# Moving the last adaLN pass of a hybrid decoder step from the key scores to S5, in half panels

## The chip, the core and the metric

One NeuronCore of a Trainium2 chip runs the whole program; the other cores are idle. The metric is device microseconds of one execution, the median of the runs. The engines are TensorE (PE, with its weight loads as PEld), VectorE (DVE), ScalarE (ACT), GpSimd (POOL) and SyncE (SP). The last two issue most of the DMAs here, POOL on queue q0 and SP on queue q1; both are worked off by the same 16 DMA engines. Everything is float32. A float32 matmul shows as two MATMUL instructions in the trace, so 8 matmuls are "x16".

## The reference

A two-layer decoder step is computed for one prompt of 256 tokens and eight samples of one token each, with width 1024 and shared weights. Layer 0 is attention (MoBA with 8 heads, and NSA with compressed, selected and window branches), layer 1 is an S5 state-space layer with a GLU. Each is followed by a squared-ReLU MLP. Each of these four sub-layers has its own conditioning:

```python
def adaln(c, w, b):
    m = (jax.nn.silu(c) @ w + b)[:, None, :]
    return jnp.split(m, 3, axis=-1)          # shift, scale, gate
def modulate(x, g, shift, scale):
    return rms_norm(x, g) * (1 + scale) + shift
def mlp_sublayer(x, c, g, ada_w, ada_b, w1, w2):
    shift, scale, gate = adaln(c, ada_w, ada_b)
    h = modulate(x, g, shift, scale)
    return x + gate * (jnp.square(jax.nn.relu(h @ w1)) @ w2)
```

Here `c` has 9 rows (prompt and samples), and each `w` is 1024 x 3072, 12 MB. Four such passes are computed, numbered 0 (attention), 1 (MLP of layer 0), 2 (S5) and 3 (MLP of layer 1). The result of pass 3 is needed only by the last MLP: by its norm, its gates and nothing earlier.

## The kernel before

The program is one straight list of instructions for each engine, ordered by hand; semaphores with counted values (class `Signals`) tie the lists together. The stages that matter here, in order, with their time in the profile:

- **MoBA values** (280 to 372 us). SP loads 64 units of 256 KB (128 rows of one cache page) into 8 slots `kv`. TensorE's `moba_pv(r)` uses 8 units a round. Behind rounds 0 to 2 stands the conditioning pass 2 (`ada(2, ...)`), between rounds 3 to 7 stand pair steps of the prompt's attention (`pair_scores`, `pair_rest`).
- **Key scores** (375 to 441 us). 24 units: 16 of selected keys (SP loads units 0, 1, 4, 5 of each 8, POOL gathers 2, 3, 6, 7), then 8 of window keys (SP, in runs of 512 bytes). For each unit n TensorE transposes (`turn_keys`), ACT evacuates, TensorE scores (`score_keys`). `beside_keys(n)` puts other work between the units.
- **Pair steps of NSA** (453 to 515 us) with values by SP, then the **output projection** (two panels, `w_out`), norm 1, and **MLP 0** (557 to 803 us).
- **S5** (803 to 877 us): norm 2 (DVE multiplies, ACT adds the shift), copies of `hT` into `U[half]`, `states_in(half)` on TensorE, then a DVE chain (`turn_in`, `states`), with `y_of(k)` on TensorE for the outputs of each half.
- **GLU** (878 to 937 us), norm 3, **MLP 1** and the output.

A conditioning pass loads six panels of 1024 x 512 (2 MB) into the ring of 4 slots, multiplies each (8 matmuls with `cT` as weights in four column groups, 32 rows each), ACT copies the row out (`ada_evac`), and 16 small matmuls turn it back into columns (`turn_back`). DVE's `mods_evac` adds the bias and gain.

Pass 3 stands in the key scores: its panels have ring numbers 28 to 33, its matmuls follow units 9, 11, 13, 15, 18 and 21 (`ADA3_AT`). POOL's queue issues in this order: pass 2's six panels, pass 3's panels 0 to 3, the gathered key units, pass 3's panels 4 and 5, the two panels of `w_out` (numbers 34 and 35), the first four MLP panels. A load waits until its slot is used: `mm_done` grows by 4 for each ring panel, and the first MLP panels wait for `4 * SEQ["w_out"]`.

In S5 the ring is cut anew: its lower half holds 4 MLP-sized panels of 1 MB (`panels`), and `PANEL` numbers them in order, w1 and w2 of layer 0, the GLU's 8, then layer 1. Panel n is loaded when panel n - 4 is used. Ahead of `states_in(0)` TensorE waits for the whole norm:

```python
normed(2)
pe.wait_ge(N.out_free, 16)
pe.wait_ge(N.s5_b_ev, 4 * LAG)
pe.wait_ge(N.s5_c_ev, LAG)
...
pe.wait_ge(N.u_dve, 1)
states_in(0)
pe.wait_ge(N.s5_b_ev, 4 * LAG + 1)
states_in(1)
```

## Time and profile before

| | |
|---|---|
| median of 3 runs | 1185.12 us (1183.18 to 1186.55) |
| the profiled execution | 1189.66 us, span 1187.9 us |
| mean granted TensorE clock | 0.908 of full speed |
| busy in the span | PE 1026.6 us (86%), DVE 421.4 (35%), ACT 252.4 (21%), POOL 121.5 (10%) |
| chain that ended last | PE 69%, DMA 11%, DVE 11%, ACT 4% |
| DMA | 215.10 MB, mean 181 GB/s |

The span runs from the first to the last instruction, and the execution's own time has some 1.8 us around it. A timeline row gives the start, the time it covers, the engine, the program line (L), the operation with its operands, the count of merged instructions, and in brackets how long the engine stood idle before it and what ended that. The chain follows the last instruction back through what released it, so it shows which of several waits counted. In a window row PEclk is the share of full clock that TensorE was granted, 1.00 for 2.4 GHz and 0.50 for 1.2 GHz. The mean DMA rate hides stages: at some the DMA engines are full, at others nearly idle.

### The profile page before, as it was taken

The page shows a single profiled execution, that of the slowest core. Times are in us where ns is not written, and L with a number is a line of the kernel's source. Part 1 is how long each engine was busy: PE and PEld are TensorE (multiplying, and loading weights), DVE is VectorE, ACT ScalarE, POOL GpSimd, SP SyncE. Part 2 cuts the span into 40 slices and gives each one's busy share as a digit, 9 for nine tenths or more (in the row PEclk, how much of TensorE's full clock was granted, in tenths as well). Part 3 has the DMA queues.
Part 4 walks back from the last instruction along what each step waited for, and adds up shares of the span by engine and source line. Part 5 has one row for each costly group of instructions (what it writes and reads, how often), then busy time and mean ns, then how long its engine had stood idle before and what let it go on. Part 6 is the DMA issues. An engine that isn't in the chain of part 4 may idle for free.

```text
span 1187.9 us, 20856 instructions
## 1 busy us (share of the span) xinstructions
PE 1026.6 (86%) x8308; PEld 748.3 (63%) x8308; DVE 421.4 (35%) x893; ACT 252.4 (21%) x546; POOL 121.5 (10%) x154
## 2 busy tenths in 40 slices
PE   4868999945878878997999999994679799999998
PEld 2556433422323545676888888884568588878886
DVE  0434049878042344533797310006931300000000
ACT  3234121102033432422213322005021211100000
POOL 2000000101103310000111111020002011111110
PEclk9779989977898875898999999997689899999999
DMA  9984549989997794303744434441014334543440
GB/s 326 340 280 130 179 156 346 354 301 376 404 341 235 251 307 140 89 19 60 259 147 136 143 135 142 142 140 39 4 47 141 108 106 144 154 159 120 162 144 36
DMA packets 106762, 215.10 MB, mean 181 GB/s; under 512 B 20464, under 2 KB 53040, under 8 KB 106585
## 3 DMA queue, kind: packets, MB, share of 16 engines
q0 software_dynamic: 38464, 147.96, 36.9%
q1 hardware_dynamic: 66314, 63.05, 16.6%
q10 hardware_dynamic: 1904, 2.94, 0.7%
q8 instruction: 60, 0.98, 0.3%
q14 instruction: 20, 0.16, 0.0%
HBM read 210.63 MB, written 7.48 MB: 184 GB/s over the span
## 4 chain that ended last, share of the span: by engine, by line
PE 69%; DMA 11%; DVE 11%; ACT 4%; SPq 2%; issue 2%; DVEq 0%; ACTq 0%; POOL 0%; POOLq 0%
PE psum L1194 20%; PE psum L1203 19%; DMA sb_arena<-in_cache_moba_kv 7%; PE psum L1386 5%; PE psum L624 4%; PE psum L772 2%; PE psum L1178 2%; PE psum L808 2%; DVE sb_sq L1932 2%; PE psum L683 2%; DVE sb_sq L1936 2%; DMA sb_arena<-in_state_nsa_win 2%; DMA sb_ring<-in_attn_ada_w 1%; PE psum L696 1%; DMA sb_arena<-in_cache_nsa_kv 1%
## 5 line engine op out<-in xcount | busy, mean ns | idle before, releaser
L1194 PE MATMUL psum<-sb_hT,sb_ring 128*128 128x264 f32 x1024 | 234.3, 392 | 13.3 <-ACT sb_hT L1433 6.8
L1203 PE MATMUL psum<-sb_arena,sb_ring 128*128 128x264 f32 x1024 | 229.1, 386 | 2.6 <-DVE sb_arena L2180 2.4
L1194 PEld LDWEIGHTS psum<-sb_hT,sb_ring 128*128 128x128 f32 x1024 | 197.7, 194 | 48.0 <-issue 6.8
L1203 PEld LDWEIGHTS psum<-sb_arena,sb_ring 128*128 128x128 f32 x1024 | 194.2, 190 | 36.3 <-issue 3.2
L624 PE MATMUL psum<-sb_cst,sb_arena 128*128 128x128 f32 (+4 forms) x457 | 77.4, 307 | 34.1 <-DMA sb_arena<-in_cache_nsa_kv 8.0
L624 PEld LDWEIGHTS psum<-sb_cst,sb_arena 128*128 128x128 f32 (+4 forms) x457 | 55.1, 154 | 54.0 <-issue 24.4
L2187 DVE SCALAR_TENSOR_TENSOR sb_xT<-psum,sb_mods,sb_xT 128x256 f32<-128x256 f32 (+1 forms) x16 | 7.7, 483 | 223.2 <-PE psum L1203 223.2
L808 PE MATMUL psum<-sb_ring,sb_hT 128*128 128x512 f32 (+1 forms) x192 | 79.4, 566 | 0.0
L683 PE MATMUL psum<-sb_ring,sb_cT 128*32 128x512 f32 x384 | 57.4, 708 | 11.3 <-DMA sb_ring<-in_attn_ada_w 10.1
L2180 DVE TENSOR_TENSOR sb_arena<-sb_arena x16 | 19.7, 1256 | 127.4 <-ACT sb_arena L1671 108.5
L808 PEld LDWEIGHTS psum<-sb_ring,sb_hT 128*128 128x128 f32 x192 | 35.5, 190 | 44.2 <-issue 39.8
L1386 PE MATMUL psum<-sb_sq,sb_ring 128*128 128x264 f32 x256 | 58.2, 386 | 1.1 <-ACT sb_sq L1712 1.1
L567 POOL DMA_DIRECT2D sb_ring<-in_mlp_w x28 | 24.8, 884 | 317.8 <-PE psum L1194 146.7
L1386 PEld LDWEIGHTS psum<-sb_sq,sb_ring 128*128 128x128 f32 x256 | 48.6, 190 | 9.5 <-ACT sb_sq L1712 1.3
L902 PE MATMUL psum<-sb_arena 128*32 128x512 f32 x128 | 43.7, 733 | 10.4 <-DMA sb_arena<-in_cache_moba_kv 10.2
L574 POOL DMA_DIRECT2D sb_ring<-in_mlp_w x32 | 28.3, 884 | 210.5 <-PE psum L1203 146.0
L1932 DVE TENSOR_TENSOR sb_sq<-sb_arena 128x512 f32<-128x512 f32 x64 | 42.0, 689 | 11.8 <-DMA sb_arena<-in_cache_moba_kv 5.6
L1936 DVE TENSOR_REDUCE sb_sq<-sb_sq 128x1024 f32 x32 | 39.0, 1220 | 4.8 <-DVE sb_sq L1932 1.3
L1848 DVE COPY sb_arena<-psum 64x256 f32<-64x256 f32 x64 | 27.3, 427 | 33.8 <-PE psum L624 32.5
L683 PEld LDWEIGHTS psum<-sb_ring,sb_cT 128*32 128x32 f32 x384 | 12.9, 124 | 37.4 <-issue 35.1
L1655 ACT COPY sb_arena<-psum 32x2048 f32<-32x2048 f32 x16 | 29.7, 1857 | 27.5 <-PE psum L624 27.2
L1671 ACT ACTIVATE sb_arena<-psum 128x264 f32 x32 | 12.5, 391 | 104.0 <-PE psum L1194 104.0
(414 smaller groups left out, 1098.6 us busy)
## 6 DMA issues: line engine op xcount, KB each, us to landing
sb_ring<-in_mlp_w POOLq DMA_DIRECT2D x64, 1024.0 KB, 6.1
sb_arena<-in_cache_moba_kv SPq DMA_DIRECT2D x128, 256.0 KB, 7.4
sb_ring<-in_mlp_ada_w POOLq DMA_DIRECT2D x12, 2048.0 KB, 13.3
sb_ring<-in_attn_ada_w POOLq DMA_DIRECT2D x6, 2048.0 KB, 22.5
sb_ring<-in_ssm_ada_w POOLq DMA_DIRECT2D x6, 2048.0 KB, 16.9
sb_ring<-in_attn_w_in POOLq DMA_DIRECT2D x5, 2048.0 KB, 11.5
sb_arena<-in_cache_nsa_kv SPq DMA_DIRECT2D x64, 128.0 KB, 2.6
sb_ring<-in_s_w_glu POOLq DMA_DIRECT2D x16, 512.0 KB, 5.3
```

The lines of the kernel that those rows point to most:

```text
L574: pool.dma_start(panels[:, j, :].rearrange("p (f c) -> p f c", f=8), w2[:, 8 * j:8 * j + 8, DS(it * 256, 256)]).then_inc(mlp_full_at[j], 16)
L624: return nc.tensor.transpose(out, in_, ident[0:rows, 0:rows])
L683: last = mm(mm_banks[i % len(mm_banks)][group(k), 0:512], cT[:, k, :], ring[:, seq % SLOTS, 512 * k:512 * k + 512], start=(k < 4), stop=(k ...
L808: last = mm(bank[3 * (p % 2) + t][:, 0:w], hT[:, k, P * t:P * t + P], ring[:, seq % SLOTS, w * k:w * k + w], start=(k == 0), stop=(k == KC ...
L902: mm(bank[5][rows, 0:512], p_of(half, r // 2, pg), kv[:, seq % KVS, :], start=(r == 0 and pg < 2), stop=(r == 7 and pg == 7)).then_inc(kv_ ...
L1194: last = mm(bank[m % 4][:, 0:T], panels[:, j, 256 * k + P * ch:256 * k + P * ch + P], hT[:, k, :], start=(k == 0), stop=(k == KC - 1))
L1203: last = mm(bank[2 * pair + c][:, 0:T], panels[:, j, 256 * f + P * c:256 * f + P * c + P], actT[:, 8 * j + f, :], start=(j == 0 and f == 0 ...
L1386: last = mm(bank[b][:, 0:T], panels[:, seq % SLOTS, 256 * k + P * zi:256 * k + P * zi + P], yT[:, k, :], start=(k == 0), stop=(k == KC - 1))
L1655: nc.scalar.copy(BT[32 * i:32 * i + 32, e].rearrange("p r k n -> p (r k n)"), psum[32 * e:32 * e + 32, 4:8, :].rearrange("p a c -> p (a c) ...
L1848: last = cp(pairs_of(n, e, 1), turned_of(n, e, 1))
L1932: tt(prod[:, 512 * (pg % 2):512 * (pg % 2) + 512], kv[:, pg, :], qb[:, DS(b, 1), :].rearrange("p b c -> p (b c)"), ALU.mult).then_inc(kv_f ...
L1936: last = red(sraw_b[:, DS(b, 1), 8 * (pg - 1):8 * (pg + 1)].rearrange("p b c -> p (b c)"), prod.rearrange("p (h d) -> p h d", d=64), AX, A ...
```

## The change

Pass 3 leaves the ring, POOL's early queue and `beside_keys`. It becomes 12 half panels of 1024 x 256 (1 MB), numbered 32 to 43 in `PANEL`, between MLP 0 and the GLU, whose numbers move up by 12. `w_out` takes ring numbers 30 and 31; the first MLP panels wait only for the end of pass 2.

TensorE's list in S5: halves 0 to 5 stand ahead of `states_in(0)`, which no longer waits for the whole norm; three turns and halves 6 to 9 stand between the samples' matmuls and `y_of(4)`; halves 10 and 11 behind `y_of(7)`; the last three turns in the GLU after its second panel. Two halves share a PSUM bank, and ACT evacuates them in pairs (`late_evac`) into rows of `work` (`late_rows`). ACT no longer makes the copies of lags 0 and 1 for the second half of `U`; DVE makes them, as it did for the first half. `mods_evac(3)` moves from the key scores' end to the GLU's end. `tmp8x` and `ss8` move within `cT`, whose columns 0 to 8 the pass still needs.

```diff
 SLOTS = 4
-SEQ = dict(ada0=0, cmp=6, cmp_p=20, ada2=22, ada3=28, w_out=34)
+SEQ = dict(ada0=0, cmp=6, cmp_p=20, ada2=22, w_out=30)
 W_IN_SEQ, ADA1_SEQ = (8, 9, 11, 13, 15, 17), (10, 12, 14, 16, 18, 19)
 W_ORDER = (0, 4, 1, 5, 2, 6, 3, 7)
-ADA3_AT = (9, 11, 13, 15, 18, 21)
-MLP_START = 36
-PANEL = dict(w1_0=0, w2_0=16, glu=32, w1_1=40, w2_1=56)
+W_OUT_START = 28
+MLP_START = 30
+PANEL = dict(w1_0=0, w2_0=16, ada3=32, glu=44, w1_1=52, w2_1=68)
...
         K3 = work[:, 0:768].rearrange("p (k d c) -> p k d c", k=8, d=LAG - 1)
+        late_rows = [work[:, 768 + 512 * (j % 4):1280 + 512 * (j % 4)] for j in range(6)]
         us = work[:, 3072:3328].rearrange("p (k e b) -> p k e b", k=8, e=4)
...
         xlast = work[:, 3968:4032]
-        ss8 = cT[:, 0, 8:16]
+        ss8 = cT[:, 0, 24:32]
         U = [sqf[:, c:c + 1024].rearrange("p (k e t) -> p k e t", k=4, e=4) for c in (1024, 0)]
...
             load_ada(SEQ["ada2"], I["ssm_ada_w"][0])
-            load_ada(SEQ["ada3"], I["mlp_ada_w"][1], 0, 4)
             selected = I["cache_nsa_kv"][0].rearrange("n p a h d -> n p (a h d)")
...
                                        ).then_inc(selected_full[u % KVS], 16)
-            load_ada(SEQ["ada3"], I["mlp_ada_w"][1], 4, 6)
             for i in range(2):
...
                 if layer == 0:
-                    pool.wait_ge(N.mm_done, 4 * SEQ["w_out"])
+                    pool.wait_ge(N.mm_done, 4 * W_OUT_START)
                     for j in range(SLOTS):
...
             load_mlp(0)
+            for i in range(12):
+                n = PANEL["ada3"] + i
+                pool.wait_ge(N.mm_done, mlp_done(n - SLOTS + 1))
+                pool.dma_start(panels[:, n % SLOTS, :].rearrange("p (k c) -> p k c", k=KC),
+                               by_rows(I["mlp_ada_w"][1])[:, :, 256 * i:256 * i + 256]).then_inc(mlp_full_at[n % SLOTS], 16)
             for i in range(8):
...
         GAINS = ((MQ, 8, 0), (MK, 8, 1), (NQ, 8, 2), (KSEL, 2, 4), (KWIN, 2, 5))
-        ADA_SEQ = tuple(tuple(SEQ[name] + i for i in range(6)) if name in SEQ else ADA1_SEQ for name in ("ada0", "ada1", "ada2", "ada3"))
+        ADA_SEQ = tuple(tuple(SEQ[name] + i for i in range(6)) if name in SEQ else ADA1_SEQ for name in ("ada0", "ada1", "ada2"))
         GAIN_AT = (96, 120, 104, 128)
...
                     last.then_inc(N.pv_done, 1)
-                if n in ADA3_AT:
-                    i = ADA3_AT.index(n)
-                    ada(3, bank[0:1], bank[7], first=i, end=i + 1)
                 if n == 19:
...
             pe.wait_ge(N.win_log, 1)
-            pe.wait_ge(N.ada_row, 6 * 4)
             for h in range(NSA_H):
...
             pe.wait_ge(N.cp_ready, 1)
-            pe.wait_ge(N.mods_ready, 4)
             pe.wait_ge(N.bias_nsa, 16)
...
-            normed(2)
+            LATE_BANK = (4, 5, 7, 0, 6, 4)
+
+            def late_half(i):
+                seq = PANEL["ada3"] + i
+                pe.wait_ge(mlp_full_at[seq % SLOTS], mlp_full(seq))
+                c = TP * (i % 2)
+                for k in range(KC):
+                    last = mm(bank[LATE_BANK[i // 2]][group(k), c:c + TP], cT[:, k, :], panels[:, seq % SLOTS, TP * k:TP * k + TP],
+                              start=(k < 4), stop=(k >= 4))
+                last.then_inc(N.mm_done, 2)
+
+            def late_turn(j):
+                pe.wait_ge(N.ada_row, 18 + j + 1)
+                for ch in range(4):
+                    for g in range(4):
+                        c = 256 + (4 * j + ch) * 9
+                        last = mm(bank[7][32 * g:32 * g + 32, c:c + 9], late_rows[j][:, P * ch + 32 * g:P * ch + 32 * g + 32],
+                                  cst[:, C_SL:C_SL + 9], start=True, stop=True)
+                last.then_inc(N.ada_tr, 1)
+
             pe.wait_ge(N.out_free, 16)
...
             pe.wait_ge(N.s5_c_ev, LAG)
+            pe.wait_ge(N.s5_b_ev, 4 * LAG + 1)
+            for i in range(6):
+                late_half(i)
...
             states_in(0)
-            pe.wait_ge(N.s5_b_ev, 4 * LAG + 1)
+            normed(2)
+            pe.wait_ge(N.u_dve, 2)
+            pe.wait_ge(N.ada_row, 18 + 3)
             states_in(1)
...
             last.then_inc(N.us_mm, 1)
+            pe.wait_ge(N.u_free, 8)
+            for j in range(3):
+                late_turn(j)
+            for i in range(6, 10):
+                late_half(i)
             pe.wait_ge(N.x_done, 8)
...
                 y_of(k)
+            pe.wait_ge(N.y_ev, 7)
+            for i in range(10, 12):
+                late_half(i)
+            pe.wait_ge(N.ada_row, 18 + 5)
             for a in range(4):
...
                     pe.wait_ge(N.fin_ev, 2)
+                    for j in range(3, 6):
+                        late_turn(j)
                 if n:
...
                     nc.scalar.copy(keysT[:, n % 2, :], bank[2 + n % 2][:, 0:512]).then_inc(N.keys_ev, 1)
-                    if n + 1 in ADA3_AT:
-                        i = ADA3_AT.index(n + 1)
-                        ada_evac(3, bank[0:1], first=i, end=i + 1)
...
             last.then_inc(N.u_ready, 1)
-            u_half(1, range(LAG))
+            def late_evac(j):
+                act.wait_ge(N.mm_done, mlp_done(PANEL["ada3"] + 2 * j + 2))
+                if j >= 4:
+                    act.wait_ge(N.ada_tr, 18 + j - 3)
+                nc.scalar.copy(late_rows[j], bank[(4, 5, 7, 0, 6, 4)[j]][:, 0:512]).then_inc(N.ada_row, 1)
+
+            for j in range(3):
+                late_evac(j)
+            u_half(1, (2, 3))
+            late_evac(3)
+            late_evac(4)
             act.wait_ge(N.y_ev, 1)
...
                 f(yT[:, k, 0:TP], yT[:, k, 0:TP], ACT.Gelu_apprx_tanh).then_inc(N.gelu_ready, 1)
+            late_evac(5)
             act.wait_ge(N.fin_tr, 1)
...
                 dve.wait_ge(N.ada_tr, 6 * (n + 1))
-                src = bank[6 if n == 2 else 7]
+                src = bank[7][:, 256:] if n == 3 else bank[6 if n == 2 else 7]
                 then(tt(mods[:, n].rearrange("p c j -> p (c j)").rearrange("p (c j) -> p c j", j=9),
...
                     then(tt(tmp8x, xs, xs, ALU.mult))
-                    red(ss8, at(cT[:, 0, 0:], (1, 8), (32, 8)), AX, ALU.add).then_inc(N.x_ready, 1)
+                    red(ss8, at(cT[:, 0, 16:], (1, 8), (32, 8)), AX, ALU.add).then_inc(N.x_ready, 1)
                     scale_samples(n + 1)
...
-            tmp8x = cT[:, :, 0:8]
+            tmp8x = cT[:, :, 16:24]
...
-            mods_evac(3)
             dve.wait_ge(N.win_log, 1)
...
             for k in range(KC):
-                static_out(0, k, 4 * SEQ["w_out"] + k + 1, bank[k % 4])
+                static_out(0, k, 4 * W_OUT_START + k + 1, bank[k % 4])
             add_samples(0, 8)
...
             nc.vector.memset(X[:, :, :, 0:1], 0.0).then_inc(N.padded_ready, 1)
+            dve.wait_ge(N.h_ready, 24)
+            for i in range(2):
+                for e in range(4):
+                    last = cp(U[1][32 * i:32 * i + 32, :, e, :], hT[32 * e:32 * e + 32, 4:8, STEPS * i:STEPS * i + STEPS])
+            last.then_inc(N.u_dve, 1)
...
                 add_out(2, glu[:, n % 2, :], n, mods[:, 2, 16 + n], tmp8x[:, n, :])
+            mods_evac(3)
             add_samples(2, 24)
```

## Rows read from the trace of the kernel before

**Rows 1.** The page, part 3: DMA queue, kind: packets, MB, share of 16 engines.
```profile
q0 software_dynamic: 38464, 147.96, 36.9%
q1 hardware_dynamic: 66314, 63.05, 16.6%
```

**Rows 2.** Windows in the MoBA values: busy us by engine, PEclk, DMA share, GB/s.
```profile
314.00:320.00 6.00, 4.84 (x51) 1.73 (x51) 0.00 (x0) 0.00 (x0) 0.00 (x0) 1.00 1.03 404
...
350.00:356.00 6.00, 4.61 (x38) 2.21 (x38) 3.72 (x9) 3.42 (x11) 0.00 (x0) 1.00 0.64 198
```

**Rows 3.** Timeline of POOL's queue (start us, us, operation), 265 to 600 us.
```profile
309.71 0.88 POOL L510 DMA_DIRECT2D sb_ring<-in_mlp_ada_w  x1 [19.86 <-PE psum L683]
...
400.16 0.90 POOL L510 DMA_DIRECT2D sb_ring<-in_mlp_ada_w  x1
...
432.99 3.52 POOL L562 DMA_DIRECT2D sb_ring<-in_mlp_w  x4 [19.53 <-PE psum L683]
```

**Rows 4.** Chain of waits, 195 to 420 us: start us, us, what.
```profile
307.87 9.37 DMA sb_arena<-in_cache_moba_kv
...
364.03 6.44 DMA sb_arena<-in_cache_moba_kv
...
407.17 20.34 DMA sb_arena<-in_state_nsa_win
```

**Rows 5.** Timeline of TensorE in the MoBA values (L902 is their matmul).
```profile
329.59 2.20 PE L902 MATMUL psum<-sb_arena 128*32 128x512 f32 x12
...
334.99 1.05 PE L902 MATMUL psum<-sb_arena 128*32 128x512 f32 x2 [1.07 <-DMA sb_arena<-in_cache_moba_kv]
...
351.65 2.13 PE L902 MATMUL psum<-sb_arena 128*32 128x512 f32 x16
```

**Rows 6.** Timeline of SP's queue in the same stretch.
```profile
340.63 23.73 SPq L412 DMA_DIRECT2D sb_arena<-in_cache_moba_kv  x24
```

**Rows 7.** Timeline of TensorE in the key scores, 383 to 441 us.
```profile
400.78 1.92 PE L683 MATMUL psum<-sb_ring,sb_cT 128*32 128x512 f32 x16
402.50 0.46 PE L673 MATMUL psum<-sb_cst,sb_hT 128*32 128x9 f32 x32
...
427.55 1.12 PE L624 MATMUL psum<-sb_cst,sb_arena 128*128 128x128 f32 x4 [2.81 <-DMA sb_arena<-in_state_nsa_win]
...
429.05 3.62 PE L683 MATMUL psum<-sb_ring,sb_cT 128*32 128x512 f32 x16
...
440.51 2.13 PE L1108 MATMUL psum<-sb_arena 64*128 64x8 f32 x32 [0.67 <-ACT sb_arena L1536]
```

**Rows 8.** Windows and timeline of TensorE in the pair steps.
```profile
470.00:480.00 10.00, 10.00 (x44) 6.27 (x44) 3.41 (x8) 3.19 (x11) 0.00 (x0) 0.50 0.29 81
...
471.99 1.97 PE L624 MATMUL psum<-sb_cst,sb_arena 128*128 128x128 f32 x8
...
481.55 1.97 PE L624 MATMUL psum<-sb_cst,sb_arena 128*128 128x128 f32 x8
...
493.46 1.09 PE L624 MATMUL psum<-sb_cst,sb_arena 128*128 128x128 f32 x8
```

**Rows 9.** Timeline of all engines in S5, 799 to 895 us.
```profile
803.62 1.75 POOL L583 DMA_DIRECT2D sb_ring<-in_s_w_glu  x2 [5.36 <-PE psum L1203]
...
814.84 0.11 DVE L2337 MEMSET sb_arena<- 128x64 f32 x1
...
816.25 6.53 PE L1318 MATMUL psum<-sb_sq,sb_arena 128*32 128x64 f32 x256 [10.95 <-ACT sb_hT L1433]
...
866.52 1.50 PE L1330 MATMUL psum<-sb_hT,sb_arena 32*32 32x192 f32 x24 [7.74 <-DVE sb_arena L2408]
...
877.55 14.51 PE L1386 MATMUL psum<-sb_sq,sb_ring 128*128 128x264 f32 x64 [1.08 <-ACT sb_sq L1712]
```

**Rows 10.** The page, part 6 (KB each, us to landing); chain at 445 us.
```profile
sb_ring<-in_mlp_w POOLq DMA_DIRECT2D x64, 1024.0 KB, 6.1
...
445.61 0.30 DVE sb_mods L1755
```

## The prediction

> **What bounds the kernel now.** I read the page first, then the chain of waits in order of time, then the timelines of TensorE, of POOL and of SP in the two stretches that the change touches, and last the granted clock by stretch. TensorE carries most of the chain, but not in the first stretch. There the values of MoBA stream in by SP while POOL's queue carries weights. The page tells how the two queues differ: POOL's q0 moved 147.96 MB in 38464 packets (3.85 KB each), SP's q1 63.05 MB in 66314 (0.95 KB each) [rows 1]. From 314 to 320 us the 16 DMA engines are full (share 1.03, 404 GB/s), while at 350 to 356 they are not (0.64) [rows 2]. What fills them is the pass that leaves: POOL issues the first ada3 panel at 309.71 and three more soon after, 2 MB each [rows 3]. The chain then runs through DMA waits for kv units: one issued at 307.87 takes 9.37 us to land, one issued at 364.03, with no weights beside it, 6.44 us [rows 4]. In the key scores it is the same: ada3's last two panels are issued from 400.16 on [rows 3], the output projection's two behind them, and the fifth window unit, issued at 407.17, lands 20.34 us later [rows 4], when TensorE has waited for it until 427.55 [rows 7]. In S5 the bound is other: TensorE stands still for 10.95 us ahead of the first states matmul, waiting for ACT, and 7.74 us ahead of the second half's outputs, waiting for DVE [rows 9]. These are the gaps that the panels go into.
>
> **Part 1, the MoBA values.** 8 MB of ada3 leave the stretch from 310 to 345. Step by step: the last unit of the third round (issued 307.87) would land in about 6.44 us as the undisturbed one does, not 9.37, so TensorE goes on 2.9 us earlier. The ada2 panels, the compressions and the first pair scores between the third and fourth round are TensorE, ACT and DVE work and move along unchanged. The fourth round's last unit is used at 334.99 + 1.05 = 336.0; a round whose units have all landed takes 2.13 us (the one at 351.65) [rows 5]. It started at 329.59 [rows 5], so without waits it would end at 331.7, 4.3 us earlier. What is late next is SP: 24 units were issued in 23.73 us, 7.9 us a round [rows 6], with the engines not full. Four more rounds at that pace are 31.6 us; before, they took from 336.0 to 371.5 (the last unit lands at 364.03 + 6.44 [rows 4] and is used in 1.05), that is 35.5. So 3.9 more. Sum: 2.9 + 4.3 + 3.9 = **11.1 us**. Low bound: 4.3, the waits of the fourth round alone. High bound: 13, if SP's pace also gains.
>
> **Part 2, the key scores.** Out go six panels, each 16 matmul instructions (1.92 us) and a turn back of 32 (0.46) at full clock [rows 7], six ACT copies, and 4 MB of ada3's loads. But POOL's queue moves up: nothing gates the output projection's two panels any more, nor the first four MLP panels (4 x 1 MB, before at 432.99 [rows 3]), since their new threshold is the end of ada2. All six are issued in some 5 us right behind the last gathered key page, at the place where ada3's fifth panel was. So q0 gets 8 MB at once where it got 8 MB panel by panel, as TensorE freed the slots: the burst is no smaller. Before, it was worked off by about 427.5, together with five window units. I take the same here, counted from the same point: the last window units land when q0 has drained, near 427. What goes is what came behind the last wait. From 427.55 to the end of the key stage, where the next stage's scores start at 440.51, were 13.0 us [rows 7]; the panel at 429.05 with its turns takes 4.7 of these. If the eighth window unit is the one that is waited for instead of the fifth, only its own unit and the four query and key turns follow, some 5 us as an estimate from the same rows. So 13.0 - 5 + 0.5 (the wait ends sooner) = **8.3 us**. Low bound 4.7, the panel alone. High bound 16: TensorE not held by windows at all; then DVE's maximum of the selected scores is late next.
>
> A rule that speaks against this part stands in the Trainium skill, DMA: Bandwidth & Descriptors, "Queues, rings and completion order": each engine alternates between its queues packet by packet. By it the small packets of the window units keep getting the same small share as long as q0 has anything to do, however the burst is made up; the trace bears it out as far as it goes (the 20.34 us). By the rule this part stays near its value above, by equal shares of the queues it would come near 13.
>
> Off DVE's chain, `mods_evac(3)` goes: the first of its two operations is 0.30 us [rows 10], with the second and the gap **0.6 us**, at 445.61, where DVE is what TensorE waits for.
>
> **Part 3, the first gap of S5.** Panels 0 to 3 follow the last MLP panels as the GLU's did: the fourth is issued at 803.62 [rows 9]. A 1 MB load lands in 6.1 us [rows 10], so at about 809.7. TensorE is free at 816.25 - 10.95 = 805.3; a half panel has the same 16 instructions as a whole one with half the columns, 0.9 us at full clock, 1.8 at half. Halves 0 to 2 run until 808, half 3 at 809.7. Panels 4 and 5 wait for their slots (halves 0 and 1) and are issued near 806.5 and 807.4, landing at about 812.6 and 814: half 5 ends near 815.5. The first states matmul no longer waits for all of the norm, only for its first half and the copies of it, ready at 814.84 [rows 9]; so it starts at about 815.5 instead of 816.25: **-0.7 us**. In order on TensorE it stands behind the halves, so a late panel costs the chain; that is the added wait. Bounds: -4 (the work keeps the clock up and the states matmuls run at full speed) and +4 (panels take half as long again). ACT's three evacuations (0.6 each) take the place of the eight copies that DVE takes over, and DVE has nothing to do there until the first states are done at 816.25 + 6.53 = 822.8: nothing, while both stay ahead of the second half's matmuls.
>
> **Part 4, the second gap and behind.** Three turns (0.46) and four halves (0.9) are 5 us in a gap of 7.74 [rows 9]: nothing; at half clock 9 to 10, which would be up to 2 us. Halves 10 and 11 come behind the last S5 output. Between it and the GLU's first matmul at 877.55 lies the last GELU, with 1.08 us idle [rows 9] beside five transposes; 1.8 us go into that: **+0.7**. Three turns more stand within the GLU, which is TensorE-bound: **+1.2**. `mods_evac(3)` ahead of the last samples' sum runs beside ACT's table load: +0.1. The GLU panels are loaded later, two of them only when halves 10 and 11 are done, yet the third and fourth are wanted 14 us and more after that, against 6 us of landing: nothing. Sum of parts 3 and 4: **+1.3 us**, from -5 to +8.
>
> **Sum.** 11.1 + 8.3 + 0.6 - 1.3 = 18.7 us gained. The profiled execution took 1189.66 us, of which the span is 1187.9; it would take 1171. The median of the runs, 1185.12, is 4.5 lower, and the same subtraction gives **1166.4 us**.
>
> **The rivals.**
> *The burst and SP's pace eat the gain.* Part 1 gives only its low bound 4.3, part 2 its 4.7 and 0.6, the rest as above: 8.3 in all, so 1177. For it: q0 gets as many bytes in the key scores as before, and SP's issue rate is a bound of its own. Against: the full DMA engines end at once when ada3 has landed.
> *More than forecast.* The windows land before the burst, the S5 matmuls find a full clock: 11.1 + 13 + 0.6 + 3 = 27.7, so 1157. For it: without ada3 the early key units free their slots sooner, so that more windows are ahead of the burst.
> *The gaps don't hold the panels.* Halves wait for their slots and hold the states matmuls, and the second gap overflows: parts 3 and 4 cost 8 instead of 1.3: 12.0 are left, so 1173.
> *The clock, on the other side.* One pair step takes 9.56 us (471.99 to 481.55) with the clock granted at 0.50, that is 1.2 GHz, for the stretch 470 to 480; at 493.46 its eight transposes take 1.09 instead of 1.97 us, and the step, by that ratio, 5.3 [rows 8]. Some three of seven steps run slow now. ada3's wide matmuls stand among the narrow key units, and without them TensorE may have more and longer pauses. If key units and all pair steps are granted 1.2 GHz: four steps more at 4.3 are 17, and 15 units, whose transposes take 1.12 at that speed [rows 7] and by the ratio 0.62 at full, are another 7.5. 24.5 against 18.7: 1191, slower. It decides from three quarters of that stretch on. The Trainium skill, TensorE: Matmul & The Clock Gate, "HAM oscillation — how this bites in real kernels", tells of kernels that start each burst slow when bursts of matmuls are short against their DMA waits; the waits for the window units are such a place.
> Against: the stretch of slow pair steps follows a pause behind 440.51 in which TensorE waits for DVE, which is there with and without ada3.
>
> **How the numbers follow.** Forecast 0.50, more than forecast 0.14, burst and pace 0.17, gaps 0.09, clock 0.10. The first four are faster: 0.90; of the last, 0.07 slower and 0.03 within 0.3% (3.6 us, about what a measurement of this kernel can tell from no change). The range goes from 1150 (both high bounds in part) to 1181 (both low bounds and S5 dear); outside are the clock and the tails.
>
> **What would show it.** Right: no weights beside the MoBA values after about 315, the output of MoBA some 11 us earlier; six loads of POOL in a row behind the gathered keys, and TensorE's last wait in the key scores still a window unit; the S5 states starting within 1 us of before, counted from the last MLP matmul; the GLU some 2 us longer from the last S5 output to the norm. Wrong: SP's rounds as slow as before, a window wait that lasts longer than 20 us, pair steps of 9.6 us to the end, or a states matmul that waits for a half panel's load.

## The result, and the profile after

| | before | after |
|---|---|---|
| median of the runs shown with the change | 1185.24 us (4 runs, 1183.18 to 1186.55) | 1199.12 us (4 runs, 1195.15 to 1204.54) |
| ratio to before, 95% interval | | 1.0122 (1.0075 to 1.0169) |
| a second series: ten runs of after | 1188.42 us (23 runs) | 1193.86 us, 1.0046 (1.0016 to 1.0077) |
| profiled execution, span | 1189.66, 1187.9 us | 1195.15, 1193.5 us |
| mean granted TensorE clock | 0.908 | 0.901 |

The forecast was 1166.4 us, faster. The kernel is slower, by 0.5 to 1.2%. The ratios, here and below, are taken against the runs of before in the same series and leave out slow executions (over 1.5% above the kernel's fastest), so they are not quotients of the medians shown.

The table below cuts each profile at the first instruction of a stage (S5: from the last matmul of MLP 0 to the first of the GLU). It holds a profile of every kernel of this study, since one profile of each of two kernels would have misled. Each row is one execution. In f4, g1 and h1 it was the fastest of the kernel's ten or twelve (1175.34 us where the median is 1184.38, 1173.52 for 1184.28, 1183.05 for 1187.5), so their rows add up to less than their medians. All in us.

| kernel | head | to values | MoBA values | key scores | cp, pair steps | out, norm 1 | MLP 0 | S5 | GLU | norm 3 | MLP 1 |
|---|---|---|---|---|---|---|---|---|---|---|---|
| before | 266.1 | 14.3 | 91.1 | 69.0 | 76.1 | 40.1 | 246.6 | 74.3 | 59.8 | 9.7 | 233.1 |
| before, again (e0) | 265.8 | 14.2 | 89.9 | 71.0 | 70.2 | 40.0 | 246.6 | 74.4 | 59.8 | 9.8 | 233.8 |
| after | 272.2 | 14.8 | 85.9 | 65.7 | 72.9 | 40.1 | 245.7 | 83.7 | 60.8 | 10.0 | 233.9 |
| after, again (g0) | 271.0 | 15.1 | 85.3 | 68.2 | 71.3 | 40.1 | 245.6 | 84.5 | 60.9 | 9.7 | 233.7 |
| e1 small loads in S5 | 266.5 | 14.6 | 85.9 | 68.8 | 77.0 | 40.0 | 246.7 | 74.0 | 60.9 | 9.7 | 234.4 |
| e2 few matmuls in S5 | 269.7 | 14.8 | 86.5 | 69.8 | 71.4 | 40.1 | 245.7 | 84.5 | 61.7 | 9.7 | 233.4 |
| e3 no pass 3 | 266.8 | 14.5 | 88.3 | 69.0 | 73.0 | 40.0 | 245.7 | 74.6 | 59.8 | 9.9 | 233.9 |
| f1 small loads in front | 272.4 | 14.6 | 86.1 | 63.9 | 68.6 | 40.0 | 246.5 | 74.5 | 59.8 | 9.7 | 232.9 |
| f2 no pass 3, held | 272.7 | 14.5 | 85.2 | 55.3 | 68.2 | 40.1 | 246.4 | 74.9 | 59.9 | 9.7 | 234.3 |
| f3 after, held | 269.7 | 15.0 | 85.2 | 56.3 | 73.0 | 40.0 | 246.4 | 83.9 | 60.9 | 9.7 | 233.7 |
| f4 before, held | 262.1 | 14.9 | 89.2 | 62.1 | 70.5 | 42.9 | 246.4 | 74.5 | 59.8 | 9.8 | 233.7 |
| g1 held and spread | 266.2 | 14.9 | 85.7 | 55.6 | 68.2 | 40.1 | 246.4 | 78.4 | 65.4 | 9.8 | 233.1 |
| h0 after, held, again | 272.2 | 14.4 | 85.7 | 56.9 | 71.3 | 40.1 | 245.6 | 83.0 | 60.8 | 9.8 | 232.7 |
| h1 held and split | 270.0 | 14.3 | 91.1 | 63.0 | 70.1 | 40.1 | 245.7 | 76.5 | 59.8 | 9.7 | 233.2 |

Three columns carry the story, and each has two levels. S5 takes 74 us, or 84 where whole half panels are loaded as after does it (g1 and h1, which load some of them there, lie between). MoBA's values take 89 to 91 with pass 3's loads, 85 to 88 without. The key scores take 62 to 71 in most, 55 to 57 in f2, f3, h0 and g1. The head (the same instructions in all) goes from 262.1 to 272.7, and the pair steps from 70.2 to 76.1 in two profiles of before alone: these two are chance.

The chain of waits of after, in order of time (start us, us, what), at the places that answer to [rows 4] and [rows 9]:

```profile
336.48 1.28 ACT L1596
...
337.77 1.87 ACT sb_arena L1596 x8
...
407.78 24.02 DMA sb_arena<-in_state_nsa_win
...
801.33 9.29 DMA sb_ring<-in_mlp_ada_w
...
816.73 3.96 issue
...
870.09 3.37 issue
```

The window unit that TensorE waits for last takes 24.02 us to land, against 20.34 [rows 4]. A half panel's load of 9.29 us is new on the chain, and so are two stretches in S5 in which TensorE waits for nothing but its own instructions ("issue").

POOL's queue in after (start us, us, operation), answering to [rows 3] and [rows 9]:

```profile
400.71 1.78 POOL L511 DMA_DIRECT2D sb_ring<-in_attn_w_out  x2
402.49 3.51 POOL L561 DMA_DIRECT2D sb_ring<-in_mlp_w  x4
...
800.46 2.63 POOL L580 DMA_DIRECT2D sb_ring<-in_mlp_ada_w  x3 [2.01 <-PE psum L1304]
805.20 0.88 POOL L580 DMA_DIRECT2D sb_ring<-in_mlp_ada_w  x1 [2.11 <-PE psum L1304]
809.64 0.89 POOL L580 DMA_DIRECT2D sb_ring<-in_mlp_ada_w  x1 [3.56 <-PE psum L1304]
812.93 0.88 POOL L580 DMA_DIRECT2D sb_ring<-in_mlp_ada_w  x1 [2.39 <-PE psum L1304]
861.00 0.88 POOL L580 DMA_DIRECT2D sb_ring<-in_mlp_ada_w  x1 [47.20 <-PE psum L1304]
863.31 0.88 POOL L580 DMA_DIRECT2D sb_ring<-in_mlp_ada_w  x1 [1.42 <-PE psum L1304]
864.19 3.51 POOL L587 DMA_DIRECT2D sb_ring<-in_s_w_glu  x4
```

Six loads, 8 MB, go out at once in the key scores, as the forecast had it. In S5 a load follows each half panel that is used, so some are always on the way while TensorE goes on to the narrow matmuls.

TensorE in after (in brackets the idle time before, and what ended it):

```profile
333.81 1.92 PE L906 MATMUL psum<-sb_arena 128*32 128x512 f32 x16
...
340.96 1.54 PE L628 MATMUL psum<-sb_cst,sb_arena 128*128 128x128 f32 x6 [3.86 <-DVE sb_arena L2079]
...
431.84 1.12 PE L628 MATMUL psum<-sb_cst,sb_arena 128*128 128x128 f32 x4 [1.03 <-DMA sb_arena<-in_state_nsa_win]
...
438.62 2.72 PE L1108 MATMUL psum<-sb_arena 64*128 64x8 f32 x23 [0.68 <-ACT sb_arena L1570]
...
807.65 1.67 PE L1304 MATMUL psum<-sb_ring,sb_cT 128*32 128x256 f32 x16 [3.17 <-DMA sb_ring<-in_mlp_ada_w]
...
820.69 2.59 PE L1339 MATMUL psum<-sb_sq,sb_arena 128*32 128x64 f32 x118 [3.96 <-issue]
...
873.46 1.71 PE L1358 MATMUL psum<-sb_arena,sb_ring 128*32 128x64 f32 x52 [3.37 <-issue]
```

At 333.81 the fourth round of MoBA's values runs through without a wait, against the two of [rows 5]. At 340.96 stands what came in their place. 816.73 to 820.69 is a hole within `states_in(0)`, and 870.09 to 873.46 one within `y_of(6)`. Both come again in g0 (3.98 and 3.62 us) and in f3 (4.07 and 3.47).

### The profile page after: what moved, and what is told of

It reads as the page before. It is cut to its first block, busy times and chain, and to the rows that moved or that the text cites. A ratio compares the mean times of both kernels' runs of the same rounds, so it can differ in the third digit from the quotient of the medians.

```text
span 1193.5 us, 21055 instructions
## 1 busy us (share of the span) xinstructions
PE 1028.0 (86%) x8404; PEld 757.7 (63%) x8404; DVE 424.1 (36%) x901; ACT 249.1 (21%) x538; POOL 127.5 (11%) x160
## 4 chain that ended last, share of the span: by engine, by line
PE 69%; DMA 11%; DVE 11%; ACT 3%; issue 3%; SPq 2%; DVEq 0%; ACTq 0%; POOL 0%
PE psum L1193 19%; PE psum L1202 19%; DMA sb_arena<-in_cache_moba_kv 5%; PE psum L1418 5%; PE psum L628 4%; PE psum L776 3%; PE psum L1177 2%; PE psum L812 2%; DVE sb_sq L1974 2%; DMA sb_arena<-in_state_nsa_win 2%; DVE sb_sq L1978 2%; DMA sb_arena<-in_attn_qk_g 2%; PE psum L906 1%; PE psum L700 1%; DMA sb_arena<-in_cache_nsa_kv 1%
## 5 line engine op out<-in xcount | busy, mean ns | idle before, releaser
L628 PE MATMUL psum<-sb_cst,sb_arena 128*128 128x128 f32 (+4 forms) x457 | 82.2, 321 | 48.2 <-DMA sb_arena<-in_state_nsa_win 9.4
L628 PEld LDWEIGHTS psum<-sb_cst,sb_arena 128*128 128x128 f32 (+4 forms) x457 | 58.6, 161 | 67.7 <-issue 24.6
L812 PEld LDWEIGHTS psum<-sb_ring,sb_hT 128*128 128x128 f32 x192 | 35.5, 190 | 44.2 <-issue 39.8
L687 PE MATMUL psum<-sb_ring,sb_cT 128*32 128x512 f32 x288 | 42.6, 697 | 11.6 <-DMA sb_ring<-in_attn_ada_w 10.4
L906 PE MATMUL psum<-sb_arena 128*32 128x512 f32 x128 | 37.3, 740 | 5.7 <-DMA sb_arena<-in_cache_moba_kv 5.7
L776 PE MATMUL psum<-sb_arena,sb_ring 128*128 128x256 f32 x128 | 30.5, 403 | 1.0 <-ACT sb_arena L1491 1.0
```

The source lines that it names most:

```text
L628: return nc.tensor.transpose(out, in_, ident[0:rows, 0:rows])
L687: last = mm(mm_banks[i % len(mm_banks)][group(k), 0:512], cT[:, k, :], ring[:, seq % SLOTS, 512 * k:512 * k + 512], start=(k < 4), stop=(k ...
L776: last = mm(bank[kind][:, 0:256], w1k[kind][:, i, :], at(pairs[:, 4096 * kind + P * i:], (2048, 2), (1, P)), start=(i == 0), stop=(i == CM ...
L812: last = mm(bank[3 * (p % 2) + t][:, 0:w], hT[:, k, P * t:P * t + P], ring[:, seq % SLOTS, w * k:w * k + w], start=(k == 0), stop=(k == KC ...
L906: mm(bank[5][rows, 0:512], p_of(half, r // 2, pg), kv[:, seq % KVS, :], start=(r == 0 and pg < 2), stop=(r == 7 and pg == 7)).then_inc(kv_ ...
```

## The experiments

**Chance, and how much (e0).** The two profiles differed by 6.1 us where nothing was changed. The kernel before, once more; no edit.

> The kernel before, unchanged, for a second profile. In the profiles of before and after the two kernels differ by 6.1 us (266.1 against 272.2 us) at the first matmul of the key gate, ahead of which no instruction was changed. Theory chance (start of the loads and clock of the first stages vary from execution to execution): this profile reaches the key gate at a time other than 266.1, by 2 us or more, anywhere from 263 to 272. Theory of a systematic loss (something in the changed kernel slows the unchanged head): 265.5 to 266.7 here, and about 272 in every kernel with the changed front.

Measured: 265.8 us to the key gate, 1184.97 us. That alone is what the systematic loss would give here, but its other half falls: e1, e3 and g1, with the changed front, have 266.2 to 266.8, and f1, h1 and f4, which load as before does up to there, 272.4, 270.0 and 262.1. So the 6.1 us are chance. So is the clock of the pair steps: e0, which is the kernel before, has 70.2 us there, not 76.1 [rows 8]. The 4.0 us that after seemed to gain there are none.

**S5: loads or matmuls (e1, e2)?** Two kernels from after, one with 1/8 of each half panel's bytes, one with 1/8 of its matmuls:

```diff
-                               by_rows(I["mlp_ada_w"][1])[:, :, 256 * i:256 * i + 256])
+                               by_rows(I["mlp_ada_w"][1])[:, 0:1, 256 * i:256 * i + 256])
...
-                for k in range(KC):
+                for k in range(1):
```

> The kernel after, with each of the 12 half-panel loads of S5 cut to its first row block (128 KB instead of 1 MB); all matmuls, turns and waits stay, on old data of the panel, so the result of pass 3 is not the reference's. After has 83.8 us from the last MLP 0 matmul to the first GLU matmul, before 74.2; 2.4 of the 9.6 are waits for landing panels, 4.0 an issue stall within states_in(0), 4.2 issue stalls within y_of(5 to 7). Theory contention (TensorE's instructions come over the same DMA engines and starve while the panels fill them): the stall in states_in(0) goes and so do the landing waits, 74 to 76 us, the time about 8 us below after, near 1190. The GLU's own loads stay, so the stalls in y_of may stay in part. Theory supply (the added narrow matmuls themselves use up what was fetched ahead): the 4.0 stall stays, 80 to 82 us, near 1197.

> The kernel after, with one of the eight matmuls of each half panel kept (16 instructions become 2); all loads, waits and turns stay, so the result of pass 3 is not the reference's. Theory contention: the stall within states_in(0) of 4.0 us stays (at least 2.5) and the waits for landing panels too, 80 to 83 us from MLP 0 to the GLU, the time 1195 to 1198. Theory supply: the stalls go, only the 2.4 of landing waits are left, 75 to 77 us, near 1190.

| | median | ratio to before (95%) | S5 |
|---|---|---|---|
| e1, few bytes, all matmuls | 1186.0 us | 1.0006 (0.9967 to 1.0045) | 74.0 |
| e2, all bytes, few matmuls | 1196.1 us | 1.0062 (1.0032 to 1.0092) | 84.5 |

TensorE in e2:

```profile
818.53 3.04 PE L1339 MATMUL psum<-sb_sq,sb_arena 128*32 128x64 f32 x127 [2.39 <-issue]
823.72 6.00 PE L1339 MATMUL psum<-sb_sq,sb_arena 128*32 128x64 f32 x217 [2.15 <-issue]
...
873.25 1.01 PE L1358 MATMUL psum<-sb_arena,sb_ring 128*32 128x64 f32 x45 [4.02 <-issue]
```

TensorE in e1, at the same two places:

```profile
810.98 5.41 PE L1339 MATMUL psum<-sb_sq,sb_arena 128*32 128x64 f32 x256 [2.99 <-DVE sb_sq L2376]
...
867.38 0.98 PE L1358 MATMUL psum<-sb_arena,sb_ring 128*32 128x64 f32 x52 [2.35 <-issue]
```

In e1 all 256 instructions of `states_in(0)` run in one piece, and the hole within `y_of(6)` is down to 2.35 us. The GLU's panels, which are still loaded whole, are what fills the DMA engines there. The matmuls of pass 3 cost nothing in the gaps: with all of them and few bytes S5 takes 74.0 us, as before (`states_in(0)` ends 2.5 us sooner behind MLP 0 than in before, and the hole in `y_of(6)` takes that back). The bytes cost the 10 us, with hardly a matmul. What stands still is a run of narrow matmuls whose instructions don't come. The profile's DMA queues show them as traffic of their own: in after, between 780 and 880 us,

```profile
q8 instruction: 18, 0.29, 1.2%
```

that is 18 packets of 16 KB. From 804 to 818 us, while data fills the engines (share 1.03), not one of them lands in after; one lands between 818.0 and 819.3, and at 820.69 the hole in `states_in(0)` is over. Even with the DMA engines idle, narrow matmuls use up a packet faster than the next arrives: in e3 (below), with no panel in flight, the samples' matmuls go in runs of 128, each followed by a pause:

```profile
825.85 1.89 PE L1369 MATMUL psum<-sb_arena 32*32 32x8 f32 x128 [2.04 <-issue]
829.30 1.89 PE L1369 MATMUL psum<-sb_arena 32*32 32x8 f32 x128 [1.56 <-issue]
```

128 matmuls and their 128 weight loads to a packet. Beside idle engines such pauses last up to 2.54 us (before, in the same matmuls), and there they cost nothing, since DVE's chain is what ends last. Beside full ones they last up to 4.07 (f3), and in `states_in(0)` and `y_of(6)` the chain goes through them. The Trainium skill, Runtime: NRT & Kernel Launch, "Instruction fetch mechanics", tells of blocks of 16 KiB and 256 instructions that the sequencer fetches through a DMA queue of its own, and says that crossing from one to the next is mostly hidden. The sizes agree with these rows; "mostly hidden" does not, where the instructions are this short.

**The front alone (e3).** After without pass 3: no loads, matmuls or turns of it anywhere, S5 as before. The last MLP's conditioning is taken from pass 2; its own is left out. The edit of after, cut to its main places:

```diff
-            for i in range(12):
-                n = PANEL["ada3"] + i
...
+            normed(2)
...
-            for i in range(6):
-                late_half(i)
...
+            cp(mods[:, 3], mods[:, 2]).then_inc(N.mods_ready, 1)
```

> The changed front alone: pass 3 is left out as a whole (loads, matmuls, turns; its conditioning is taken from pass 2, so the last MLP's result is not the reference's), S5 and GLU are as before the change. By the two profiles the front gains 5.2 (MoBA values) + 3.3 (key scores) + 4.0 (pair steps at full clock) + 1 (MLP 0) = 13.5 us less 0.3 behind the key scores. Theory chance for the head: 1185 - 13 = 1172, from 1168 to 1176. Theory of a systematic loss of 6 us in the head: 1178 (1176 to 1181). If the gain by clock in the pair steps is chance too: 4 us more in either case. My forecast of 20 us for the front would give 1165.

Measured: 1184.53 us, 1.0015 of before (0.9975 to 1.0055). Only a loss of 6 us in the head with 4 us on top would have given that (up to 1185), and the head takes 266.8 us here, as in before; so the gain of the front is what is missing. Six panels gone for good, and the key scores still take 69.0 us. TensorE in e3:

```profile
412.23 1.12 PE L623 MATMUL psum<-sb_cst,sb_arena 128*128 128x128 f32 x4 [1.30 <-DMA sb_arena<-in_state_nsa_win]
...
418.82 1.11 PE L623 MATMUL psum<-sb_cst,sb_arena 128*128 128x128 f32 x4 [3.47 <-DMA sb_arena<-in_state_nsa_win]
...
425.43 1.11 PE L623 MATMUL psum<-sb_cst,sb_arena 128*128 128x128 f32 x4 [4.33 <-DMA sb_arena<-in_state_nsa_win]
...
428.69 1.11 PE L623 MATMUL psum<-sb_cst,sb_arena 128*128 128x128 f32 x4 [1.60 <-DMA sb_arena<-in_state_nsa_win]
```

10.7 us of waits for window units, where before has 2.8 and pass 3's matmuls. These matmuls had been work beside a wait. That is not all of the 69.0: the granted clock is 0.51 over the stage in this profile, against 0.62 in after, and TensorE is busy for 52.6 us against 46.6 with the same matmuls.

**What makes the windows late (f1 to f4).** f2, f3 and f4 put one wait into POOL's list, in e3, after and before; f1 is before with pass 3's six panels cut to their first row block.

```diff
+            pool.wait_ge(N.keys_tr, 24)
             for i in range(2):
                 load(SEQ["w_out"] + i, by_rows(I["attn_w_out"][0])[:, :, 512 * i:512 * i + 512])
```

> The kernel before, with each of pass 3's six panels cut to its first row block (256 KB instead of 2 MB); its matmuls, turns and copies stay between the key units, on old data, so the result of pass 3 is not the reference's. With pass 3 left out as a whole the key scores took 69.0 us (before: 69.0 and 71.0 in two profiles) with the clock at 0.50 from 375 to 450, and MoBA's values 88.3 (91.1 and 89.9). Theory clock: pass 3's wide matmuls among the key units keep the clock up (0.7 and more from 395 to 440), and its loads cost time; with the loads gone and the matmuls kept the key scores fall to 60 to 64 us, the time to 1172 to 1178. Theory loads do not matter: key scores 68 to 71, MoBA 88 to 91, the time within 4 us of before.

> The kernel without pass 3 (S5 and GLU as before the change; the last MLP's result is not the reference's), with POOL waiting for the last key unit's transposes before it loads the output projection and the first four MLP panels. Without this wait TensorE stood still for 10.7 us in four waits for window units between 411 and 429, the last of which landed 23.7 us after its issue beside 8 MB of these loads. Theory burst: the window units land in under 10 us, the waits go, the key scores take 57 to 61 us instead of 69, the time is 8 to 12 us below that kernel's 1184.5, so 1173 to 1177. Theory clock alone (half speed sets the pace of the key units whatever lands): key scores 65 to 69, time 1181 to 1185.

> The kernel after, with the same wait of POOL before the output projection's loads. Theory burst: as much as in the kernel without pass 3, 8 to 12 us below after (1199.1 in its first runs), so 1187 to 1191; what is left above the kernel without pass 3 and with the wait is S5's 10 us. Theory clock alone: 1195 to 1199.

> The kernel before, with the same wait of POOL before the output projection's loads; pass 3 stays in the key scores. Before, 4 MB of the output projection came between pass 3's last panels and the window units; TensorE waited 2.8 us for a window unit and 4.4 us for instructions (issue) in that stretch. Theory burst: these waits go in part, key scores 63 to 67 us instead of 69 to 71, the time 1180 to 1183 against 1186. Theory that pass 3's own last panels are what holds the windows: key scores 68 to 71, time unchanged. The output projection is loaded later and still wanted 80 us after: no cost there.

| | median | ratio to before (95%) | key scores |
|---|---|---|---|
| f1 before, few bytes | 1178.48 us | 0.9928 (0.9897 to 0.9959) | 63.9 |
| f2 no pass 3, held | 1173.95 us | 0.9876 (0.9828 to 0.9924) | 55.3 |
| f3 after, held | 1182.99 us | 0.9944 (0.9908 to 0.9981) | 56.3 |
| f4 before, held | 1184.38 us | 0.9994 (0.9968 to 1.0019) | 62.1 |

DMA issues in the key scores (count, KB each, median us to landing), first after:

```profile
sb_ring<-in_attn_w_out POOLq DMA_DIRECT2D x2, 2048.0 KB, 14.3
sb_ring<-in_mlp_w POOLq DMA_DIRECT2D x4, 1024.0 KB, 22.9
sb_arena<-in_state_nsa_win SPq DMA_DIRECT2D x8, 256.0 KB, 11.8
```

and f3, after with POOL's wait:

```profile
sb_ring<-in_attn_w_out POOLq DMA_DIRECT2D x2, 2048.0 KB, 12.2
sb_ring<-in_mlp_w POOLq DMA_DIRECT2D x3, 1024.0 KB, 21.2
sb_arena<-in_state_nsa_win SPq DMA_DIRECT2D x7, 256.0 KB, 3.8
```

The burst is the cause: a window unit lands in 3.8 us instead of 11.8, and the key scores shrink by 9 to 12 us (65.7 and 68.2 in after and g0, 56.3 and 56.9 in f3 and h0), by one wait that TensorE never feels. TensorE is busy for 44.9 to 46.6 us in all four, so what goes is idle time and not a slow clock. Between e3 and f2 it is otherwise: of the 13.7 us some 9 are busy time (52.6 and 43.3 us), at a clock of 0.51 and 0.72. f1 shows the same for pass 3's own panels: cut to 1/8, with all matmuls kept, they let the windows land in 4.0 us instead of 15.0, and no wait for them is left. Its key scores are in the range of the first theory, but as the windows are early too, it doesn't show that the clock is what is gained. f2 came out as the burst theory had it, f3 4 us below. f4 gains 7 to 9 us in the key scores by its profile, but its runs as a whole show no difference; its profile is that of its fastest run, and where the gain went in the others stays open. f3 has the lowest ratio of the kernels here that compute the whole reference. What limits it next is DVE: TensorE in f3, at the maximum of the selected scores,

```profile
410.87 1.62 PE L629 MATMUL psum<-sb_cst,sb_arena 128*64 128x128 f32 x6 [3.81 <-DVE sb_arena L2008]
```

**Towards a version that beats both (g1, g0, h1, h0).** g1 is f3 with pass 3 spread so that no panel should be in flight beside narrow matmuls that count: halves 4 to 7 in the second gap, 8 to 11 between GLU panels 2 to 5, and two holds in POOL's list.

```diff
+HALF_SEQ = (32, 33, 34, 35, 36, 37, 38, 39, 43, 45, 47, 49)
+GLU_SEQ = (40, 41, 42, 44, 46, 48, 50, 51)
...
+                    if i == 4:
+                        pool.wait_ge(N.u_mm, 1)
...
+                if i == 1:
+                    pool.wait_ge(N.y_mm, 7)
```

> The kernel after with POOL's wait in the key scores, and pass 3 spread anew so that no panel is in flight while the end waits for narrow matmuls: halves 0 to 3 ahead of the first states matmul, halves 4 to 7 in the second gap with their loads held until the first states matmuls are done, halves 8 to 11 between the GLU's panels 2 to 5, and of the GLU's own loads only the first ahead of the last S5 output (the others wait for it). The result is the reference's. Theory contention: the issue stalls within the first states matmuls and within the outputs of the second half go, 74.5 to 77 us from MLP 0 to the GLU instead of 83.9; the GLU pays 4 half panels and turns, 64 to 66 instead of 60.9; in all 3 to 6 us below after with the wait (1183.0), 1177 to 1180. Theory that the gaps don't hold the panels in any case: 79 us or more up to the GLU, and 1182 to 1186.

> The kernel after, unchanged, on the same chip as the spread version. Theory that it is slower by S5's 9.5 us and gains nothing in front: 1193 to 1199, 0.8% above before. Its head up to the key gate, where nothing was changed, took 272.2 us in its first profile and from 262.1 to 272.7 in the profiles of ten kernels with the same head: by chance, anything in that range.

g1: 1184.28 us, 0.999 (0.9962 to 1.0018); S5 78.4 and GLU 65.4, together 143.8 against 144.8 in f3. TensorE in g1:

```profile
794.43 0.35 PE L1348 MATMUL psum<-sb_sq,sb_arena 128*32 128x64 f32 x9 [0.56 <-issue]
...
837.17 0.76 PE L1322 MATMUL psum<-sb_cst,sb_arena 128*32 128x9 f32 x43 [2.42 <-issue]
...
837.79 6.36 PE L1313 MATMUL psum<-sb_ring,sb_cT 128*32 128x256 f32 x62
```

The hole in the first states matmuls is gone (0.56 instead of 3.96 us). But in the second gap four halves take 6.36 us, most of it at half clock (0.56 from 838 to 844), and overrun it, and the GLU takes 5.6 us more than in before: what was saved in one place was paid in two others, and the 3 to 6 us below f3 that were expected did not come. g0 repeats after: 1193.86 us, 1.0046 (1.0016 to 1.0077), at the low end of what was expected.

h1 leaves four panels between the key units and moves only the last two, as four half panels, into the first gap; h0 is f3 on the same chip. The edit of h1 against before, cut to its main places:

```diff
-ADA3_AT = (9, 11, 13, 15, 18, 21)
+ADA3_AT = (9, 11, 13, 15)
...
-            load_ada(SEQ["ada3"], I["mlp_ada_w"][1], 4, 6)
+            pool.wait_ge(N.keys_tr, 24)
...
+            for i in range(4):
+                n = PANEL["ada3"] + i
```

> Only the part of pass 3 that the first gap of S5 holds is moved there: panels 0 to 3 stay between the key units, panels 4 and 5 become four half panels ahead of the first states matmuls; nothing of pass 3 is left for the second gap or the GLU but two turns, and POOL waits for the last key transposes before the output projection's loads. The result is the reference's. Theory (a window unit waits only for what is loaded beside it, a narrow matmul only for what is loaded beside it): key scores 57 to 60 us, MoBA's values 88 to 91 as before, 74.5 to 76.5 us from MLP 0 to the GLU and 60 in the GLU: 9 to 12 us less than before by stages, so 1176 to 1180, and below after with the wait by 3 to 5. Theory that pass 3 costs the same 8 to 10 us wherever it stands: 1182 to 1186.

> The kernel after with POOL's wait alone, again, beside the split version on one chip. First time 1183.0 us, 0.994 of before. By the stages of its profile: key scores 56 us, 84 us from MLP 0 to the GLU. Expected 1181 to 1185.

h1: 1187.5 us, 1.0015 (0.9987 to 1.0044). h0: 1183.0 us, 0.9976 (0.9948 to 1.0005). In h1 the windows land in 3.4 us and S5 takes 76.5, both as wanted, but the key scores take 63.0 instead of 57 to 60. TensorE in h1:

```profile
423.55 1.62 PE L631 MATMUL psum<-sb_cst,sb_arena 128*64 128x128 f32 x6 [3.91 <-DVE sb_arena L2005]
```

Four panels with their turns stand ahead of the selected maximum, and with the windows early it is this chain that ends last, so now they count. MoBA's values are at 91.1 again. By the stages 4 to 5 us below before would be left, but the runs show no difference, and the expected 9 to 12 us are missed. The best version is f3, after with the one wait: 0.994 and 0.998 of before in two series, a quarter to half a per cent, though the interval of the second still holds no gain at all.

## Why the prediction was wrong, point by point

**Part 1, MoBA values, -11.1.** The direction was right, the size was 4.3: the other kernels without these loads beside the values (e1 to e3, f1 to f3, h0 and g1; f3 and h0 are one kernel), together with both profiles of after, average 86.0 us, the four with them (before twice, f4, h1) 90.3. The first two terms came as worked out: in after the third round ends earlier and the fourth runs without a wait. Counted from the first matmul of the values, the fourth round ends at 48.7 us instead of 55.6, 6.9 us sooner where 7.2 were forecast. The step that failed is "What is late next is SP", with the 3.9 us that follow from it. Late next is the pair step between the rounds: DVE, then ACT's table load and its exponentials (1.28 and 1.87 us on the chain), then DVE again, while TensorE stands still for 3.86 us. The fifth round begins only 1.1 us sooner than in before, and SP, which needs its slots, waits 3.7 us with it. In before this chain ran beside the waits for the fourth round's units [rows 5], so that the 4.3 us of waits were not all that ended there. A wait was priced as if nothing else was using it. The 3.9 itself was no gain to be had: it sets 31.6 us of SP's issuing at before's own pace against 35.5 us that also hold the landing and the use of the last unit (6.44 + 1.05). In after these four rounds take 37.1.

**Part 2, key scores, -8.3.** Measured -3.0 (69.0 and 71.0 against 65.7 and 68.2). POOL's six loads in a row came, and TensorE's last wait is for a window unit, both as said. (The sum itself has a slip: 13.0 - 5 + 0.5 is 8.5.) What failed is "The burst is no smaller ... I take the same here", taken as neutral: the last wait ended 31.1 us after the first of POOL's loads (400.71 to 431.80), where 27 were taken, and 6.8 us followed at half clock instead of 5. The burst was the term that decided the stage, and f3 shows how far: one wait in POOL's list, and the stage falls from 65.7 to 56.3. Taking pass 3's matmuls out brought little, since they had filled such waits. The high bound of 16, "TensorE not held by windows at all; then DVE's maximum ... is late next", is what f3 measures (-13.7, with that very DVE wait of 3.81 us), but it takes a wait in POOL's list that the change doesn't have. The rule of the Trainium skill, DMA: Bandwidth & Descriptors, "Queues, rings and completion order", which was weighed there, agrees with the trace in its direction: beside the large loads the units land in a median of 11.8 us, without them in 3.8. The 8.3 us that it was taken to leave did not come. The 0.6 us of `mods_evac(3)` can't be read beside pair steps that vary by 6.

**Part 3, the first gap, -0.7.** Measured +4.7 up to DVE's chain. The step that failed is "A 1 MB load lands in 6.1 us": that was the median of the MLP's loads, issued one by one, here several overlap and one takes 9.3, so the states matmuls start 2.4 us later. The high bound of +4 held that. The other half is the hole of 3.96 us in which instructions don't come, less the 1.6 us by which the states matmuls themselves got shorter (4.95 us on the chain instead of 6.58). It had no term: the loads were costed where data is waited for, not as traffic beside the instructions.

**Part 4, the second gap and the GLU, +2.0.** Measured +5.7, of which 3.4 and 0.9 are stalls within `y_of(6)` and `y_of(7)`, 0.15 and 0.78 in e3, beside halves 10 and 11 and the GLU's first panels. "The GLU panels are loaded later ... nothing" is the step that failed: they were early enough for the GLU and too early for the outputs ahead of it (with them alone loaded whole, e1 has 2.35 us there). Halves 10 and 11 and the turns in the GLU cost about what was worked out. By the table parts 3 and 4 come to 10.4 us in the first pair of profiles and 11.2 in the second (e0 and g0), against 1.3, beyond the bound of 8.

**The rivals.** "The gaps don't hold the panels" had the right place and nearly the price (8 us), but in the main by another mechanism: it named slots and overflow, and only the 2.4 us of late panels are of that kind; the rest is instructions. "The burst and SP's pace eat the gain" had the first half of the truth. "The clock" had a little of it: from 412 to 432 us TensorE is granted 0.50 in both profiles of after, 0.77 and 0.67 in those of before. But it isn't what made the kernel slower: the key scores got shorter all the same, the pair steps vary as much within before alone, and f3 is 9 us shorter than after in the key scores with TensorE busy nearly as long. The sum of the rivals was never weighed: the front at its low bounds (4.3, 4.7 and 0.6) and the gaps at their dear end of 8, both at once, leave 1.6 us, so 1183.5, which is already above the end of the range, 1181, that is said to hold this case. Two of the signs of being wrong came: a window unit that takes longer than 20 us, and a states matmul behind a half panel's load. By the stages of the profiles, two of each kernel for the last two terms, the change makes -4.3 - 3.0 + 10.8 = +3.5 us. The second series (1.0046, that is 2 to 9 us) holds that; the first (9 to 20 us) does not, and what it had on top stays open.

## What to carry to other kernels

Before work is taken out from beside a wait, take the wait away, or nothing is gained: find what is loaded beside the awaited transfer and hold what isn't wanted yet, since a large load with 100 us to spare can hold a small one that is wanted now. A gap of TensorE is free for matmuls, and not for their loads where short matmuls follow: hold the loads until these are through. And profile the kernel before twice before a difference of a few us between two profiles is read as an effect.

## What the runs showed of the hardware

Instructions arrive as 16 KB packets over the same DMA engines as the data (q8, 61 packets in after). In runs of narrow matmuls TensorE pauses for up to 2.54 us beside idle engines and for up to 4.07 us where panels keep these busy. A window unit of 256 KB in runs of 512 bytes lands in 3.8 us (median, f3) where the large loads are held, and beside 8 MB of them in 11.8 (after) to 16.4 us (e3), at most 24.0. The same instructions of the first 266 us took from 262.1 to 272.7 us in 14 profiles.
